# Two value outputs and the second conv value in PSUM banks outside the ring; ScalarE splits two more slabs before it copies the shifted inputs

## The reference

```
# latent attention: keys and values come from a normed latent of 256
kv = rms_norm(ckv) @ ukv_w        # 16 heads x (128 keys + 128 values)
# second block
z = rmsnorm(h) @ w_in             # queries, keys/values, gates, conv, merge gates
kc = gelu(blocks(kv[0]) + pos_k ...) @ ...   # each compressed key from 32 tokens, stride 16
c = c_val * sigmoid(c_gate)       # then a causal depthwise convolution of 31 taps
```

## Time and profile before

| | |
|---|---|
| median of 3 runs | 891.61 us (890.43 to 893.21) |
| the profiled execution | 891.58 us, its span 889.8 us |
| PE busy | 864.0 us, 97% |
| POOL busy | 627.0 us, 70% |
| DVE busy | 565.7 us, 64% |
| ACT busy | 484.0 us, 54% |
| DMA | 138.85 MB, mean 156 GB/s |

### The profile page before, as it was taken

One profiled execution on the slowest core, in us unless ns is written; L12 is line 12 of the kernel. 1 busy time (PEld: TensorE's weight loads), 2 busy tenths in 40 slices (PEclk: granted clock), 3 DMA queues, 4 the chain that ended last, 5 costly groups with the idle time before them and its releaser, 6 DMA issues.

```text
span 889.8 us, 18240 instructions
## 1 busy us (share of the span) xinstructions
PE 864.0 (97%) x7027; PEld 827.0 (93%) x7027; DVE 565.7 (64%) x1550; ACT 484.0 (54%) x919; POOL 627.0 (70%) x280
## 2 busy tenths in 40 slices
PE   7999999999999999999999999999999999999995
PEld 6999988889998899999999989888999999999994
DVE  5997757773243567677358997765556666641165
ACT  6654465664546456563755467665554444554351
POOL 3899755555997456473979798453777888889680
PEclk9999999999999999999999999999999999999997
DMA  8577633332775343443657576232565666667511
GB/s 318 183 214 218 187 116 96 96 95 51 217 226 152 116 143 105 134 119 96 184 172 213 166 207 205 87 120 71 167 169 173 190 180 186 183 191 220 181 48 48
DMA packets 38534, 138.85 MB, mean 156 GB/s; under 512 B 4272, under 2 KB 4272, under 8 KB 38448
## 3 DMA queue, kind: packets, MB, share of 16 engines
q1 hardware_dynamic: 38448, 137.69, 51.6%
HBM read 136.63 MB, written 1.05 MB: 155 GB/s over the span
## 4 chain that ended last, share of the span: by engine, by line
PE 74%; DVE 5%; POOL 4%; ACT 2%; issue 2%; DVEq 0%; ACTq 0%
PE ps L581 20%; PE ps L582 20%; PE ps L583 20%; POOL wl L533 4%; PE ps L931 2%; PE ps L802 1%; PE ps L626 1%; PE ps L955 1%; PE ps L608 1%; ACT wh L1047 1%; PE ps L826 1%; PE ps L798 1%; PE ps L708 1%; PE ps L775 1%; PE ps L944 1%
## 5 line engine op out<-in xcount | busy, mean ns | idle before, releaser
L533 POOL TENSOR_TENSOR wl<-raw,wh 128x1024 fp32r<-128x1024 f32 x254 | 611.4, 2434 | 221.7 <-ACT wh L1047 221.5
L581 PE MATMUL ps<-uh,wh 128*128 128x256 f32 x1248 | 353.8, 283 | 6.5 <-DVE ul L1544 2.7
L582 PE MATMUL ps<-ul,wh 128*128 128x256 f32 x1248 | 349.3, 280 | 0.0
L583 PE MATMUL ps<-uh,wl 128*128 128x256 f32 x1248 | 348.8, 279 | 0.0
L1047 ACT ACTIVATE wh<-raw 128x1024 fp32r<-128x1024 f32 x256 | 264.6, 1054 | 86.7 <-PE ps L583 83.2
L581 PEld LDWEIGHTS ps<-uh,wh 128*128 128x128 f32 x1248 | 235.0, 188 | 11.8 <-issue 3.3
L582 PEld LDWEIGHTS ps<-ul,wh 128*128 128x128 f32 x1248 | 235.1, 188 | 0.0
L583 PEld LDWEIGHTS ps<-uh,wl 128*128 128x128 f32 x1248 | 234.6, 188 | 0.0
L1702 DVE TENSOR_TENSOR h<-ps,h 128x256 f32<-128x256 f32 x32 | 13.6, 424 | 106.5 <-PE ps L583 106.3
L582 PE MATMUL ps<-ffl,wh 128*128 128x256 f32 x176 | 49.3, 280 | 0.0
L581 PE MATMUL ps<-ffh,wh 128*128 128x256 f32 x176 | 49.1, 279 | 0.0
(11 more groups left out here) (359 smaller groups left out, 1761.1 us busy)
## 6 DMA issues: line engine op xcount, KB each, us to landing
raw<-slabs SPq DMA_DIRECT2D x256, 512.0 KB, 4.0
h<-x_fm SPq DMA_DIRECT2D x4, 256.0 KB, 6.4
out_fm<-outb SPq DMA_DIRECT2D x4, 256.0 KB, 2.2
cst<-shape_consts SPq DMA_DIRECT2D x1, 768.0 KB, 8.8
vec<-vectors SPq DMA_DIRECT2D x1, 303.5 KB, 3.9
pin<-p_fm SPq DMA_DIRECT2D x1, 256.0 KB, 5.5
```

What stands on the lines that cost most here:

```text
L533: nc.gpsimd.tensor_tensor(wl[:, s % PART_RING, :], raw[:, s % RAW_RING, :], wh[:, s % PART_RING, :].bitcast(f32), ALU.subtract).then_inc(s ...
L581: nc.tensor.matmul(res, w_h, a_h, start=first, stop=False)
L582: nc.tensor.matmul(res, w_h, a_l, start=False, stop=False)
L583: ins = nc.tensor.matmul(res, w_l, a_h, start=False, stop=last)
```

## The change

Three edits. First, `output_banks` gives some outputs a bank of their own (`OWN_BANK`): the second output of v1 and of v3 go to bank 6 (it holds `y` of the state-space heads before and the attention of even heads after), and cv1 goes to bank 5 (scores of odd heads before). These outputs leave the ring; the others go on taking turns in `ps0` to `ps2`, and each waits for the last one in its own bank. Second, PE waits for the last readers of the two banks, `gated` 16 ahead of v1 and `prob_norm` 16 ahead of cv1. Third, ACT calls `feed("nq3")` where it called `feed("nq1")`.

```diff
+OWN_BANK = {("v1", 1): 6, ("v3", 1): 6, ("cv1", 0): 5}
...
+def output_banks(jobs):
+    ring, bank, left_by = 0, [], []
+    for j in jobs.values():
+        for t in range(j.n_out):
+            own = OWN_BANK.get((j.name, t))
+            if own is None:
+                own, ring = ring, (ring + 1) % PROJ_BANKS
+            left_by.append(max((o for o, b in enumerate(bank) if b == own), default=None))
+            bank.append(own)
+    return bank, left_by
...
                 for o in range(j.out, j.out + j.n_out):
-                    if o >= PROJ_BANKS and k0 == 0:
-                        who, n = freed[o - PROJ_BANKS]
+                    if left_by[o] is not None and k0 == 0:
+                        who, n = freed[left_by[o]]
                         wait(pe, f"{who}_evac", n)
-                outs = [psum[(j.out + t) % PROJ_BANKS] for t in range(j.n_out)]
+                outs = [psum[bank[j.out + t]] for t in range(j.n_out)]
...
             for n in range(4):
+                if n == 1:
+                    wait(pe, "gated", SSM_PAIRS)
                 project(f"v{n}", tile_of(ckh), tile_of(ckl), parts_ready(n_kv) if n == 0 else None)
...
+                if i == 1:
+                    wait(pe, "prob_norm", MLA_H)
                 project(f"cv{i}", u, u_lo)
...
-            feed("nq1")
+            feed("nq3")
             act.wait_ge(sem("cmp_x"), 1)
             nc.scalar.activation(cxh[:], cx[:], ACT.Copy).then_inc(sem("cmp_hi"), 1)
```

More of the change, by code:

```diff
@@ L251, in build @@
     jobs, freed, done_with, releases, n_slabs = plan()
+    bank, left_by = output_banks(jobs)
     VC, n_vec = vector_columns()
@@ L1055, in output @@
                 act.wait_ge(sem("proj_done"), o + 1)
-                return psum[o % PROJ_BANKS]
+                return psum[bank[o]]
             def square(n, k):
@@ L1175, in _ @@
                 wait(act, "dve_evac", freed[jobs[f"sz{j - 2}"].out][1] if j >= 2 else 0)
-                nc.scalar.activation(zb[:, j % 2, :], psum[jobs[f"sz{j}"].out % PROJ_BANKS][:, 0:T], ACT.Tanh, scale=0.5)\
+                nc.scalar.activation(zb[:, j % 2, :], psum[bank[jobs[f"sz{j}"].out]][:, 0:T], ACT.Tanh, scale=0.5)\
                     .then_inc(sem("z_tanh"), 1)
@@ L1677, in _ @@
                 wait(dve, "gated", j - 1)
-                stt(szb[:, j % 2, :], zb[:, j % 2, :], 1.0, psum[jobs[f"sz{j}"].out % PROJ_BANKS][:, 0:T],
+                stt(szb[:, j % 2, :], zb[:, j % 2, :], 1.0, psum[bank[jobs[f"sz{j}"].out]][:, 0:T],
                     ALU.add, ALU.mult).then_inc(sem("dve_evac"), 1)
```

## The result

| | before | changed |
|---|---|---|
| median | 891.92 us (890.3 to 895.63, 21 runs) | 894.99 us (891.35 to 898.65, 20 runs) |
| ratio, 95% interval | | 1.0028 (1.0017 to 1.0040) |
| profiled execution | 891.58 us, span 889.8 us | 891.35 us, span 889.6 us |

By the ratio the change costs 2.5 us (interval 1.5 to 3.6); the two medians are 3.1 us apart. (One more run of the changed kernel, 1051.66 us at a clock of 0.749, is left out; with it the median is 895.02.) The profiled execution of the changed kernel is the fastest of its runs, so its total says nothing; it has to be read stage by stage. For that I took the start of each of PE's 7027 matmuls in both traces, both counted from PE's first matmul, and followed the difference. It is a ruler that shows at which place time is lost, and it is used in the experiments too.

What follows compares the result with a forecast made beforehand. PE was busy 864.0 of 889.8 us, but DVE and then POOL set the pace from 485 to 540. 891.6 plus 1.9 (+2.9 - 1.0), plus 0.2 for the clock, gave 893.7 us; range 890.0 to 895.4.

Steps and rivals of the forecast that it cites:

- Edit 1: At v1 and v3, one output each into bank 6: v2 and v3 start without a gap, 1.0 us gained.
- Edit 2: cv1 into bank 5: it starts right behind the spread's matmuls, 1.22 us gained.
- Edit 3, the cost: Building `cx`: additions held by POOL's slabs; DVE takes nq1 3.2 us later, PE stands 3.4 us before ks.
- case A: At `cxl`: DVE gets there before POOL and saves 0.4 us; whole change +1.9 us; chance 0.45.
- list of signs: What would show it, including five `cx` additions of about 2.4 us and a group of 10.5 to 11 us.
- C: Building `cx`: POOL and DVE share, additions are not held, the third edit gives nothing: 889.4 us; chance 0.15.
- half: Building `cx`: two additions get in between two POOL slabs, PE keeps only Edit 1: 890.6 us; chance 0.12.
- Its gain: POOL's hole at 491 is filled but comes back before hk's third slab, split behind vsw's copy: 0 gained.
- Case B: At `cxl`: POOL is first, `cxl` waits 2.4 us more, chain ends about 4.4 late: 895.0 us; chance 0.20.
- The clock: PE's pause before ks may drop the granted clock to 0.50; 0 to 0.5 us reaches the end, 0.2 added.
- one addition per slab: Building `cx`: an addition waits until the running POOL instruction has ended, and POOL then starts its next slab.

Runs made afterwards that it cites:

- PSUM kernel: Changed kernel with `ce` in two resting PSUM banks instead of SBUF: 888.78 us (ratio 0.9962), again 888.82 (0.9947); without the third edit 890.85 (0.9984).
- halves: Changed kernel with POOL's low-part slabs from nq0 to nq3's limit cut in two: 897.55 us, ratio 1.0064.
- fillers: Changed kernel with 24 more matmuls into a resting bank ahead of ks: 896.55 us, ratio 1.0053; again 895.21 us, ratio 1.0013.

## Why the prediction was right

*Edit 1: right.* Predicted -1.0; the ruler steps by 0.99 to 1.00 us in all twelve profiles of kernels that have it.

*Edit 2: right.* Predicted -1.22; -1.19 to -1.20 in the same twelve.

*Edit 3, the cost: right, mechanism and size.* The held additions were predicted as a group of 10.5 to 11 us (10.82), with PE's pause 3.4 (3.10), ending in case A with `cxl` at 2.3 (2.29). The list of signs was wrong in one point, five additions of about 2.4 us: four came, since the first began 0.3 us before a slab ended and took 0.47. The working itself had that short first one (from 484.9, with a slab ending at 482.9 + 2.38), which is why its group is right. From cv1 on, A stood for +4.1 us; the rows have 4.0. The whole sum was +1.9 and the profile has +1.8. Rivals C and half fell with the group's length; the PSUM kernel shows the cause, and the halves the unit in which it is paid.

*Its gain: right.* It was counted as 0, since POOL's hole would come back behind the copy of vsw's output; it did (4.29 us at 503), and the PSUM kernels give the same with and without edit 3.

*Case B: right as a case; that A came in the first profile was close to luck.* B didn't come in the three profiles of the changed kernel, but in two others that hold the additions, at 5.3 us in place of 4.1 with fillers, where 1.5 more was forecast. In the changed kernel's first profile DVE was 0.10 us ahead of POOL, as the working had it, and in the filled kernel it was 0.09 behind once and 0.10 ahead once. In the other two profiles of the changed kernel the clock had fallen, and DVE was 0.5 ahead: the clock turns B into A, as was forecast.

*The clock: the added 0.2 had the right reason for being small.* It fell in four of the five profiles with a pause of 2.5 us or more and lost 1.5 to 2.8 us there, of which the waits behind took back nearly all (0.04 us left in the one pair of profiles that can be compared).

*Where the sum may be short.* +2.1 was forecast, a ratio of 1.0024; the ratios of the changed kernel, 1.0028, 1.0038 and 1.0021, are 1.9 to 3.4 us, and 1.0024 lies in the interval of each. The median of 895.0 lies in the range that the prediction gave to case B, which no profile of the changed kernel shows: what makes up the 0.4 us (by the ratio) to 1 us (by the medians) between the forecast and the runs is open. The profiles have executions at +1.8 and, with the addition that lost four slabs, at +2.9, which the prediction had no case for ("one addition per slab"). How often that comes isn't known from three profiles.

The Trainium skill (GPSIMD Engine Reference, Key points) speaks of contention on the SBUF interfaces shared by GpSimd and VectorE for instructions with two SBUF inputs. The PSUM kernel agrees with its condition (0.27 us with one such input, 2.48 with two). That section leaves open who gives way, and the prediction's remark is about that section alone. The traces show the one that comes second waiting: an addition to the end of POOL's instruction, and once of several, and POOL's slab to the end of `cxl` when `cxl` was first.

## What to carry to other kernels

Before filling a gap of GpSimd, look at what VectorE does in that gap: instructions with both inputs in SBUF were cheap only because GpSimd rested, and each now pays up to a whole GpSimd instruction, and once in the profiles here several. Such work gets one operand in PSUM if a bank rests (0.27 us in place of 2.48 here), or is put into fewer, wider instructions. The three output banks outside the ring paid in full where they stand (1.0 and 1.2 us), and with them alone 0.2 of the 2.2 us was lost again from 464 to 535. The fast kernels here are those with none or only two additions held: 888.8 (twice) and 890.9 us with `ce` in PSUM, 889.4 and 890.1 with the banks alone; the runs do not separate them.

## What the runs showed that was not expected

- An addition can lose every boundary between GpSimd's instructions: 9.87 us for one of 128x120, in one of three profiles of the same program.
- In the head loop, far from the change, the same collision comes in some profiles and not in others. Timeline of DVE and POOL in the PSUM kernel and then with the banks alone:
```profile
405.61 2.64 DVE L1785 TENSOR_TENSOR ogl<-ogt,ogh 128x256 fp32r<-128x256 f32 x1
...
408.17 2.57 DVE L1820 SCALAR_TENSOR_TENSOR mzb<-mze,mzb 128x256 f32<-128x256 f32 x1
```
```profile
405.58 4.88 POOL L548 TENSOR_TENSOR wl<-raw,wh 128x1024 fp32r<-128x1024 f32 x2 [4.58 <-ACT wh L1066]
```
```profile
405.77 0.75 DVE L1785 TENSOR_TENSOR ogl<-ogt,ogh 128x256 fp32r<-128x256 f32 x2
406.43 2.62 DVE L1820 SCALAR_TENSOR_TENSOR mzb<-mze,mzb 128x256 f32<-128x256 f32 x1
```
```profile
406.08 5.20 POOL L548 TENSOR_TENSOR wl<-raw,wh 128x1024 fp32r<-128x1024 f32 x2 [4.58 <-ACT wh L1066]
```
  In both POOL's slab is recorded 0.02 to 0.03 us ahead of the second `ogl`, close to a tie. In the first `ogl` lost it and was held; in the second it got through, and POOL's two slabs took 0.32 us longer. The price on the ruler from 400 to 440 is 1.7 us, or 3.5 to 3.7 where the clock fell to 0.50 behind it; it was there in six of the fourteen traces, the PSUM kernels' three among them, whose profiled executions are thus not their fastest. Whether it changes from one execution of a program to the next is not shown: of the programs profiled more than once, the PSUM kernel and the filled one have it in both profiles, the changed kernel in none of three and the banks alone in neither of two.
- From about 30 to 72 us PE's back-to-back matmuls of 128x256 begin 0.1133 us apart in some executions and 0.1178 in others, at a granted clock of 1.00 in both, so one execution is 1.6 us ahead there. Groups of line 581 before and 596 after, from 31 to 71 us:
```profile
L581 PE MATMUL ps<-uh,wh 128*128 128x256 f32 x114 | 31.9, 280 | 0.0
```
```profile
L596 PE MATMUL ps<-uh,wh 128*128 128x256 f32 x118 | 32.7, 277 | 0.0
```
  Four more of each line's matmuls fit into the same 40 us. It is not the change's: three of the thirteen profiles after before's have it, one of them without edit 3, and the changed kernel's third has not. What decides it, no run here tells.
